# Gate columns of two mixers: narrow split products with x as the stationary side, in place of column-group products summed by a second product

## What is computed

```
def _mixer_odd(h, w_in, b_f, w_out):          # FOX
    z = h @ w_in                               # (256 x 1024) @ (1024 x 3088)
    q, k, v = ...                              # 16 heads of 64 each
    zf = z[..., 3 * hd:]                       # the last 16 columns: one gate a head
    return _fox_attention(q, k, v, zf, b_f) @ w_out

def mlstm_mixer(h, w_in, b_gate, g_head, w_out):
    proj = h @ w_in
    ...
    gates = proj[..., 2 * A_QK + 2 * A_V:] + b_gate    # 16 columns: 8 input, 8 forget gates
    i_log = gates[..., :A_HEADS]
    f_log = jax.nn.log_sigmoid(gates[..., A_HEADS:])
```

## Time and profile before

| | |
|---|---|
| runs of the kernel | 1707.48, 1707.70, 1708.83 us; median 1707.7 |
| the profiled execution | 1707.48 us, of which the span from first to last instruction is 1705.7 |
| TensorE (PE) matmul busy | 1590.9 us, 93% |
| VectorE (DVE) busy | 1049.9 us, 62% |
| ScalarE (ACT) busy | 823.6 us, 48% |
| granted TensorE clock, mean | 0.969 of full |

### The profile page before, as it was taken

The page is one execution under the profiler, slowest core; times in us unless marked ns, Lnnn a source line. Parts: engine busy times, 40 slices in busy tenths (PEclk is TensorE's granted clock), DMA queues, the critical chain, the costliest instruction groups (busy, mean ns, idle before and its releaser), DMA issues.

```text
span 1705.7 us, 24040 instructions
## 1 busy us (share of the span) xinstructions
PE 1590.9 (93%) x9356; PEld 1377.4 (81%) x9356; DVE 1049.9 (62%) x1242; ACT 823.6 (48%) x985; POOL 40.5 (2%) x63
## 2 busy tenths in 40 slices
PE   6999895899999999999999998968999999899998
PEld 5888794688888888789788886957888879688887
DVE  5566678666667566655666666545566664565665
ACT  4444544545445444545554455443544453654443
POOL 6000000000000000000000000000000000000000
PEclk9999986899999999999999999979999999999999
DMA  7555542265656565464265654524555554145552
GB/s 243 192 191 180 183 135 76 75 216 176 200 172 198 174 201 179 161 198 149 75 221 175 205 177 155 179 74 157 189 177 192 193 189 161 50 161 185 193 177 98
DMA packets 197253, 284.86 MB, mean 167 GB/s; under 512 B 8816, under 2 KB 149136, under 8 KB 197184
## 3 DMA queue, kind: packets, MB, share of 16 engines
q1 hardware_dynamic: 193488, 271.09, 48.8%
q0 software_dynamic: 3552, 12.28, 2.2%
q10 hardware_dynamic: 144, 0.52, 0.1%
HBM read 282.81 MB, written 1.05 MB: 166 GB/s over the span
## 4 chain that ended last, share of the span: by engine, by line
PE 85%; DVE 8%; ACT 4%; issue 2%; DMA 1%; DVEq 0%; POOL 0%; POOLq 0%; ACTq 0%
PE ps L1484 39%; PE ps L1555 21%; PE ps L1558 11%; PE ps L1474 10%; DVE mx L1168 2%; DVE w_lo L982 1%; ACT shared L842 1%; PE ps L1504 1%; DVE xn L1004 1%; DVE xt L1041 1%; PE ps L1760 1%; ACT xt L665 1%; PE ps L1731 1%; DVE x_res L1008 1%; DMA gain<-in_norm_g_dram 1%
## 5 line engine op out<-in xcount | busy, mean ns | idle before, releaser
L982 DVE TENSOR_TENSOR w_lo<-raw,w_hi 128x2048 fp32r<-128x2048 f32 x257 | 588.0, 2293 | 386.2 <-ACT w_hi L621 386.2
L621 ACT CAST w_hi<-raw 128x2048 fp32r<-128x2048 f32 x257 | 489.2, 1907 | 126.6 <-PE ps L1484 58.2
L1555 PE MATMUL ps<-xt,w_hi 128*128 128x512 f32 x1536 | 418.2, 394 | 0.0
L1555 PEld LDWEIGHTS ps<-xt,w_hi 128*128 128x128 f32 x1536 | 265.9, 189 | 38.2
L1558 PEld LDWEIGHTS ps<-xt,w_lo 128*128 128x128 f32 x1536 | 235.5, 189 | 32.4
L1558 PE MATMUL ps<-xt,w_lo 128*128 128x256 f32 x1536 | 244.1, 281 | 0.0
L1484 PE MATMUL ps<-xt,w_hi 128*128 128x256 f32 x1600 | 228.3, 286 | 4.7 <-issue 2.4
L1484 PEld LDWEIGHTS ps<-xt,w_hi 128*128 128x128 f32 x1600 | 209.9, 194 | 6.7 <-issue 2.6
L1474 PE MATMUL ps<-w_hi,xt 128*128 128x512 f32 (+1 forms) x576 | 186.0, 406 | 24.7 <-DVE xt L1041 12.4
L1484 PE MATMUL ps<-w_hi,ht_hi 128*128 128x512 f32 x528 | 163.9, 391 | 0.0
L1484 PE MATMUL ps<-w_lo,ht_hi 128*128 128x512 f32 x528 | 163.2, 390 | 0.0
(11 more groups left out here) (204 smaller groups left out, 1263.2 us busy)
## 6 DMA issues: line engine op xcount, KB each, us to landing
raw<-in_ffn_w_gate_dram SPq DMA_DIRECT2D x132, 512.0 KB, 4.0
raw<-in_ffn_w_up_dram SPq DMA_DIRECT2D x132, 512.0 KB, 5.0
raw<-in_ffn_w_down_dram SPq DMA_DIRECT2D x132, 512.0 KB, 4.2
raw<-in_fox_w_in_dram SPq DMA_DIRECT2D x24, 512.0 KB, 4.6
raw<-in_a_w_in_dram SPq DMA_DIRECT2D x24, 512.0 KB, 4.5
raw<-in_w_kv_dram SPq DMA_DIRECT2D x16, 512.0 KB, 4.9
raw<-in_ab_w_in_dram SPq DMA_DIRECT2D x14, 512.0 KB, 4.7
gain<-in_norm_g_dram POOLq DMA_DIRECT2D x12, 512.0 KB, 3.9
```

The source lines that it names most:

```text
L621: nc.scalar.copy(w_hi[slot][:, :], raw[slot][:, :]).then_inc(hi_made, 1)
L982: nc.vector.tensor_tensor(w_lo[slot][:, :], raw[slot][:, :], w_hi[slot][:, :].bitcast(F32), ALU.subtract).then_inc(lo_made, 1)
L1555: nc.tensor.matmul(ps[:, GU_LOOP + b, :], w_hi[slot][:, col[b]], xt[:, kb, :], start=kb == 0, stop=False)
```

## The change

`zw` shrinks to its 16 columns and is split as the other weights are: at the head of `norms` of the two mixers, ScalarE makes `zw_hi` and VectorE `zw_lo`. In the step `gates` TensorE runs `three` with blocks of x stationary and 16 columns of `zw_hi` or `zw_lo` passing, for each token tile and each of the 8 blocks, into two banks with tokens in partitions; ScalarE copies `z` straight from there. `z_rows`, `by_32`, `z_by_token` and the cleared columns go. GpSimd's second load of `zw` waits for the splits of the first, not for its product.

```
-        zw = sb("zw", [P, KB, 32])
-        by_32 = sb("by_32", [P, 32])
-        z_rows = junk[:, 0:S]
+        zw = sb("zw", [P, KB, 16])
+        zw_hi = sb("zw_hi", [P, KB, 16], F32R)
+        zw_lo = sb("zw_lo", [P, KB, 16], F32R)
...
-            const(nc.gpsimd.memset(zw[:, :, 16:32], 0.0))
...
-                        pool.wait_ge(gates_made, GATES[FOX] + 1)
+                        pool.wait_ge(zw_split, 2)
                         pool.wait_ge(lf_made, 1)
                         gate_columns(MLSTM)
...
             def norms(s):        # ScalarE
+                if s.get("loads") in (FOX, MLSTM):
+                    act.wait_ge(zw_landed, 32 * (1 + (s["loads"] == MLSTM)))
+                    nc.scalar.copy(zw_hi[:, :, :], zw[:, :, :]).then_inc(zw_split, 1)
...
                 elif form == "gates":        # ScalarE
                     act.wait_ge(gates_made, GATES[m] + 1)
-                    linked()
-                    nc.scalar.copy(z_rows, ps[:, b0, 0:S]).then_inc(z_rows_made, 1)
-                    act.wait_ge(gates_made, GATES[m] + 2)
-                    done = nc.scalar.copy(z[:, :, :], ps[:, b0 + 1, 0:32].rearrange("p (t c) -> p t c", t=T))
+                    done = nc.scalar.copy(z[:, :, :], ps[:, b0:b0 + 2, 0:16])
...
             def norms(s):        # VectorE
+                if s.get("loads") in (FOX, MLSTM):
+                    dve.wait_ge(zw_split, 2 * (s["loads"] == MLSTM) + 1)
+                    nc.vector.tensor_tensor(zw_lo[:, :, :], zw[:, :, :], zw_hi[:, :, :].bitcast(F32),
+                                            ALU.subtract).then_inc(zw_split, 1)
...
-                nc.vector.reduce_sum(by_32[:, :], ident[:, :].rearrange("p (g c) -> p c g", g=4), AX_X)\
-                    .then_inc(by_32_made, 1)
...
                 if form == "gates":        # TensorE
-                    pe.wait_ge(consts_made, N_CONST)
-                    pe.wait_ge(zw_landed, 32 * (1 + (m == MLSTM)))
-                    for n, (first, xs) in enumerate(itertools.product((0, 4), (xt_hi, xt_lo))):
-                        for g in range(4):
-                            ins = nc.tensor.matmul(ps[32 * g:32 * g + 32, b0, 0:S], zw[:, first + g, :],
-                                                   xs[:, first + g, :].bitcast(F32), start=n == 0, stop=n == 3)
+                    pe.wait_ge(zw_split, 2 * (1 + (m == MLSTM)))
+                    for t in range(T):
+                        for kb in range(KB):
+                            ins = three(ps[:, b0 + t, 0:16], *x_blocks(kb, t), zw_hi[:, kb, :], zw_lo[:, kb, :],
+                                        kb == 0, kb == KB - 1)
                     ins.then_inc(gates_made, 1)
...
-                                if kb == 1 and steps[steps.index(s) - 1]["form"] == "gates":
-                                    z_by_token(m, 4 - b0)
```

More of the change, by code:

```diff
@@ L21 @@
-import itertools
 from contextlib import ExitStack
@@ L64 @@
 O_BLOCK = {SWA: 4, FOX: 0, REL: 0}
-GATES = {FOX: 0, MLSTM: 3}
+GATES = {FOX: 0, MLSTM: 2}
 LF_STEPS = 4
 MAX_REL_1 = 256
-N_CONST = 29
+N_CONST = 28
 N_ONES = 5
@@ L313, in program @@
         aug_made = sem("aug_made")
-        z_rows_made = sem("z_rows_made")
-        by_32_made = sem("by_32_made")
+        zw_split = sem("zw_split")
         lf_step = sem("lf_step")
@@ L508, in gate_columns @@
             def gate_columns(m):
-                pool.dma_start(zw[:, :, 0:16], rows(IN_W[m], 0, KB, IN_COL[m, "z"], 16)).then_inc(zw_landed, 16)
+                pool.dma_start(zw[:, :, :], rows(IN_W[m], 0, KB, IN_COL[m, "z"], 16)).then_inc(zw_landed, 16)
                 bias = A["fox_b_f"][0] if m == FOX else A["a_b_gate_2"][0]
@@ L803, in proj @@
                     act.wait_ge(gates_made, GATES[m] + 1)
-                    linked()
-                    nc.scalar.copy(z_rows, ps[:, b0, 0:S]).then_inc(z_rows_made, 1)
+                    done = nc.scalar.copy(z[:, :, :], ps[:, b0:b0 + 2, 0:16])
+                elif form == "sums":
                     act.wait_ge(gates_made, GATES[m] + 2)
-                    done = nc.scalar.copy(z[:, :, :], ps[:, b0 + 1, 0:32].rearrange("p (t c) -> p t c", t=T))
-                elif form == "sums":
-                    act.wait_ge(gates_made, GATES[m] + 3)
                     done = nc.scalar.copy(c_rows[:, :], ps[:, b0, 0:S])
@@ L1626, in ffn @@
                 down_block(q + 1, 1, 1, 0, stop=True).then_inc(piece_used, 1)
[L1628 to L1635, removed]
             def proj(s):
```

## The result

The changed kernel takes 1720.2 us (median of 4 runs, 1719.5 to 1720.9), the kernel before beside it 1707.7 (1707.5 to 1708.8). The ratio is 1.0072 [1.0054, 1.0090]: 12.3 us slower, with an interval of 9.2 to 15.4. The prediction was 1713.3, with 1711.6 to 1716.6 as its range; the time lies above it. The sign held; the size is a little over twice the 5.6 us forecast.

What follows compares the result with a forecast made beforehand. TensorE was taken to bound the kernel at the gates of both mixers. Profiled 1707.48 us plus 5.68 for the products and 0.1 for the splits gave 1713.26, stated as 1713.3, range 1711.6 to 1716.6.

Steps and rivals of the forecast that it cites:

- rival 1: Clock falls in the narrow gate train, 3 to 6 us on top in both mixers: 1716.3 to 1719.3; chance 0.09.
- The sum: Profiled 1707.48 us plus 5.68 for TensorE's products and 0.1 for the splits in both mixers: 1713.26 us.
- the kv step: SWA mixer: the same helper's six products against 128 columns take 0.112 us each, at full clock, TensorE busy throughout.
- the two rows: Clock evidence: half clock from 721 to 727 us after TensorE was busy 1.31 of 3.4; full through the kv step.
- The price of the products: Gate step, each mixer: 48 narrow products at 0.112 us take 5.38 us against 2.54 before, net +2.84.
- Rival 2: Narrow gate products load faster, so the kernel isn't slower: 1707.6 us at 0.053 us a product; chance 0.06.
- The two splits: Head of the norms: ScalarE's copy hidden, VectorE's subtraction about 0.29 us, of which 0.05 a mixer shows.
- Nothing waits for zw or zw_split: Norms and GpSimd: zw lands long before MLSTM's norms; zw_split's wait replaces gates_made's, met before lf_made; no cost.
- lf has 10.7 us to spare: Behind the gates: lf's slack of nearly 6 us before it is wanted grows to 9; no wait is created.
- the stop for vt: Behind the gates: TensorE's next stop, 0.43 us for the copy of vt, moves along and pays nothing back.
- Rival 3: Later work absorbs part of the delay through the weight ring; one mixer's added time gone gives 1710.4; chance 0.05.

Runs made afterwards that it cites:

- cover first: Changed kernel with 12 narrow products ahead of the next projection and three lots of 12 behind its first three wide groups: 1713.7 us, ratio 1.0029.
- zw stationary: Changed kernel with the 32 columns of zw_hi and zw_lo stationary and all 512 columns of xt passing, 8 wide products: 1707.7 us, ratio 0.9997.
- two trains: Changed kernel with 24 narrow products ahead of the next projection and 24 behind its first half: 1714.7 us, ratio 1.0041.
- among wide: Changed kernel with the 48 products in four lots of 12 behind the next projection's first four wide groups: 1714.1 us, ratio 1.0028.
- hi only: Changed kernel with only the 16 hi by hi products a mixer, so z lacks its fine part: 1704.2 us, ratio 0.9975.

## Why the prediction was wrong

**The step that failed** is the one under rival 1 of the prediction, where the forecast took the full clock for the train (chance 0.80 against 0.09). The sum's missing term is 3.2 us a mixer: the granted clock is 0.50 for 6.8 us from inside the train on, in both mixers and both profiles. The prediction saw that the train "has an instruction under way all the time, as the kv step has, but passes an eighth of its columns; no stretch of the trace is like it", and then weighed the two rows by how busy TensorE was. The runs show that busy is not what tells these cases apart. TensorE was busy throughout with 16, with 64 and with 128 columns a product; the clock fell with the first two and held with the third. The kv step, which gave the price of the loads, passes 128 columns, and 256 in every third product: it was the right row for the load and the wrong one for the clock. That the columns passed decide is shown for the train of 48 alone; with trains of 24 the clock fell behind two of four that were alike.

**The rival had the mechanism and the size.** It worked out 3 us a mixer for 6 us at half clock, from 0.46 us for a wide product; measured are 3.2 for 6.8, and a wide product there takes (743.55 - 741.70) / 4 = 0.46. Its 1719.3 lies between the two medians of the changed kernel, 1718.4 and 1720.2. What it lacked is that a load slows too, from 0.112 to 0.213 us, so that the train pays as well (1.01 us) and not just what follows it. (The Trainium skill, "TensorE: Matmul & The Clock Gate", Part 1, says that activity releases the clock. The prediction left open whether so thin a train counts. If activity is read as TensorE being busy, these traces do not agree: it was busy for 4.00 of 4.00 us, and then had a granted clock of 0.50.)

**Held:**
- The price of the products, 48 in 5.38 us. At full clock the starts are 0.112 us apart behind the train's first two, the train of 128 columns took 5.31 us, and with it a mixer costs 2.80 us more than before, where the sum had 2.84. Rival 2 (faster loads) is out, since no train keeps a pace under 0.11. (Nor did the faster load of "Weight-path perf modes", on that page of the Trainium skill, show for this type: 0.112 us, where the prediction's estimate by it was 0.056.)
- The two splits: 0.29 and 0.28 us, both beside other work. The sum gave VectorE's 0.05 a mixer; 0.01 shows.
- Nothing waits for zw or zw_split, lf has 10.7 us to spare, the stop for vt is 0.44 us.
- Rival 3: nothing is absorbed at the gates. Behind them no saving that belongs to the change can be told: S2 and S3 together are 942.9 and 942.8 us with 128 columns and cover first, 941.1 to 941.9 before, and 940.2 and 937.1 in the changed kernel, whose S3 had less time at half clock.

**What stays open.** The stages of the two mixers give +12.0 us for the changed kernel, and the runs +12.3 and +10.1. For 128 columns it is +5.6 and +5.6, for cover first +5.8 and +5.0, for zw stationary +1.0 and -0.5, for 64 columns +12.0 and +9.4 (6.7 to 12.0), for two trains +8.9 and +7.0 (4.4 to 9.4): all within the intervals. Two are not: among wide has +8.8 by stages and +4.8 (3.2 to 6.7) timed, hi only -1.5 and -4.3 (-6.2 to -2.4). S1 to S3 vary by such amounts, and S3 goes with the time at half clock, so the likely place is where the clock's other falls come to lie once the mixers' stages have moved them. That is only argued: hi only's two profiled executions (1707.3 us for the span of 1705.5, and 1707.9) are both above its timed median, and neither shows the gain. Nor is it shown why two of the four trains of 24 brought a fall and two did not, whether 16 columns with idle gaps would do the same, or whether a train of 128 columns would hold the clock somewhere else.

No order of the work tried here that computes the gates in full beats the kernel before. The nearest, with zw stationary, equals it.

## What to carry to other kernels

A train of small matmuls has two prices. The first is the pace of its loads, which here depended on the number of stationary blocks and not on whether 16 or 128 columns passed, so count blocks, and let the narrow operand stand (8 products here, against 48). The second comes later, a third of it in the train's end and two thirds on the wide products behind it: read the granted clock in a row of the same width before taking "busy throughout" for "full clock". And before moving such work, ask what it covers: here it hid 1.3 us of another engine's copy.

## What the runs showed of the hardware

- A TensorE busy for 100% of a stretch can still lose its clock. It did so 3.4 to 4.5 us into a train of 48 products of 16 or of 64 columns (in both mixers of three profiles). With trains of 24 it came behind two of four, 1.3 and 0.2 us after their end. With 128 columns (two trains of 48, one profile) it did not happen, nor with 16 products in one train (four trains) or in lots of 12 among wide ones.
- At half clock the pace of narrow products, which their weight loads set, falls like that of wide ones: 0.213 against 0.112 us, 0.46 against 0.228.
- Falls last 6.8 or 3.4 us in these stages.
- Executions of one kernel on one chip differ in stages that have the same instructions: S1 by 3.0 us in the two later profiles of before. Over the 14 profiles S3 goes with its own time at half clock; which of the two follows from the other is not shown.
